# A three-stage transformer block in split fp32: the projections' first place from x without its tokens' scales, both norms' scales applied where it is emptied

## The reference

```python
    return rmsnorm(x, final_g)            # the end of first_block
...
def rms_norm(x, g):
    y = xf * lax.rsqrt(jnp.mean(xf * xf, axis=-1, keepdims=True) + NORM_EPS) * g.astype(jnp.float32)
...
        h = rms_norm(x, norm_mix_pre[l])
        proj = h @ w_in[l]
        q, k, v, p = jnp.split(proj, (D_ATTN, D_ATTN + D_KV, D_ATTN + 2 * D_KV), axis=-1)
...
        p_prev = jnp.concatenate([jnp.zeros_like(p[:, :1]), p[:, :-1]], axis=1)
        p = p + (p_prev - p) * rwkv_shift_mix[l]
```

## Time and profile before

| what | us |
|---|---|
| median of 3 runs | 2027.43 (2027.31 to 2029.51) |
| the profiled execution | 2027.34 |
| its span | 2026.0 |
| TensorE busy | 1829.3 (90% of the span) |
| VectorE busy | 1046.8 (52%) |
| ScalarE busy | 639.8 (32%) |
| GpSimd busy | 88.4 (4%) |
| granted TensorE clock, mean | 0.936 of full |

### The profile page before, as it was taken

One profiled execution on the slowest core, in us unless ns is written; L12 is line 12 of the kernel. 1 busy time (PEld: TensorE's weight loads), 2 busy tenths in 40 slices (PEclk: granted clock), 3 DMA queues, 4 the chain that ended last, 5 costly groups with the idle time before them and its releaser, 6 DMA issues.

```text
span 2026.0 us, 21412 instructions
## 1 busy us (share of the span) xinstructions
PE 1829.3 (90%) x8828; PEld 1473.9 (73%) x8828; DVE 1046.8 (52%) x1316; ACT 639.8 (32%) x786; POOL 88.4 (4%) x87
## 2 busy tenths in 40 slices
PE   5659999999997899999969979985599999999997
PEld 3238888887776688888857768874478888888885
DVE  4874674477426543244344574435566552466533
ACT  2124312421321342133224423432344431244422
POOL 2400010010000000000000120100000000000000
PEclk8769999999997899999988989997799999999997
DMA  9713464365321132232312240002122332332321
GB/s 357 266 63 112 155 225 153 103 209 197 94 83 42 62 105 91 96 104 84 104 62 73 63 115 8 4 1 62 42 83 87 101 104 84 103 104 84 104 83 42
DMA packets 123920, 208.55 MB, mean 103 GB/s; under 512 B 13885, under 2 KB 48341, under 8 KB 123824
## 3 DMA queue, kind: packets, MB, share of 16 engines
q1 hardware_dynamic: 115360, 174.94, 26.4%
q0 software_dynamic: 7792, 29.43, 4.4%
q10 hardware_dynamic: 672, 2.82, 0.4%
HBM read 204.01 MB, written 4.73 MB: 103 GB/s over the span
## 4 chain that ended last, share of the span: by engine, by line
PE 85%; DVE 10%; ACT 2%; issue 1%; DMA 1%; SPq 1%; DVEq 0%; ACTq 0%
PE bank L514 73%; DVE ada_acc L1569 2%; DMA ada_ring<-in_ada_w 1%; PE bank L843 1%; PE bank L530 1%; PE bank L826 1%; PE bank L806 1%; PE bank L525 1%; DVE gT L1852 1%; SPq L461 1%; DVE outer L1850 1%; PE bank L888 0%; PE bank L655 0%; DVE tmp L1531 0%; PE bank L867 0%
## 5 line engine op out<-in xcount | busy, mean ns | idle before, releaser
L1494 DVE TENSOR_TENSOR w_lo<-raw,w_hi 128x2048 fp32r<-128x2048 f32 x138 | 319.9, 2319 | 541.6 <-ACT w_hi L1103 541.6
L1103 ACT ACTIVATE w_hi<-raw 128x2048 fp32r<-128x2048 f32 x138 | 263.9, 1913 | 634.7 <-PE bank L514 611.2
L514 PE MATMUL bank<-h_hi,w_hi 128*128 128x512 f32 x736 | 292.5, 397 | 11.1 <-DVE h_lo L1541 7.7
L514 PE MATMUL bank<-u_hi,w_hi 128*128 128x512 f32 x768 | 300.5, 391 | 0.8 <-DVE conv L2047 0.8
L514 PE MATMUL bank<-u_hi,w_lo 128*128 128x512 f32 x768 | 299.0, 389 | 0.0
L514 PE MATMUL bank<-u_lo,w_hi 128*128 128x512 f32 x768 | 298.8, 389 | 0.0
L514 PE MATMUL bank<-h_lo,w_hi 128*128 128x512 f32 x736 | 290.2, 394 | 0.0
L514 PE MATMUL bank<-h_hi,w_lo 128*128 128x512 f32 x736 | 289.8, 394 | 0.0
L514 PE MATMUL bank<-f_hi,w_hi 128*128 128x512 f32 x512 | 200.3, 391 | 2.7 <-DVE f_lo L1544 2.4
L514 PE MATMUL bank<-f_lo,w_hi 128*128 128x512 f32 x512 | 199.7, 390 | 0.0
L514 PE MATMUL bank<-f_hi,w_lo 128*128 128x512 f32 x512 | 199.7, 390 | 0.0
(11 more groups left out here) (328 smaller groups left out, 2029.2 us busy)
## 6 DMA issues: line engine op xcount, KB each, us to landing
raw<-in_mlp_w SPq DMA_DIRECT2D x128, 512.0 KB, 4.6
raw<-in_w_ffn_up SPq DMA_DIRECT2D x64, 512.0 KB, 4.7
ada_ring<-in_ada_w POOLq DMA_DIRECT2D x24, 1024.0 KB, 5.8
ada_ring<-in_ada_w SPq DMA_DIRECT2D x9, 2048.0 KB, 13.9
raw<-in_w_ffn_down SPq DMA_DIRECT2D x32, 512.0 KB, 4.4
raw<-in_w_in SPq DMA_DIRECT2D x20, 512.0 KB, 4.4
raw<-in_sgu_w_in SPq DMA_DIRECT2D x16, 512.0 KB, 4.8
x_rows<-in_ada_w SPq DMA_DIRECT2D x3, 2048.0 KB, 12.9
```

Source lines behind the costliest of these rows:

```text
L514: mm = te.matmul(bank[:, n], a, b, start=first and k == 0 and j == 0, stop=last and k == 3 and j == 2)
L1103: se.activation(m.ring(s)[0], m.raw[:, slot], ACT.Copy).then_inc(sem("hi_made"), 1)
L1494: ve.tensor_tensor(lo, m.raw[:, slot], hi.bitcast(F32), ALU.subtract).then_inc(sem("lo_made"), 1)
```

## The change

Place 0 reads x * g1 * g2, split into h_hi and h_lo (`gained_hi`, `gained_lo`) as the MLP's last tiles are finished, and so needs neither scale. Squares of x and of x * g1 are summed side by side in that time (`second_square`, `add_second_square`, into the space of rstd_diag). Both means come after three quarters of slab 76 (`two_means`), the product of both scales is worked out in rows of four and spread inside slab 77 (`scale_spread`), and VectorE empties place 0 with it into bT (`scaled_out`), from which ScalarE and VectorE do the shift. For places 1 to 4, h is rebuilt over h_hi and h_lo from x, the gains and the product of scales; place 1 is now the one with k outermost. The first scale alone is spread in slab 78 and kept, and the rewriting of xT by NORM_FINAL (x_final) is done in the mixer's eight units.

The lora matrices get a place of their own and are loaded at the end of the MLP. `blocks(1)` comes in the middle of slab 82. The blocks are stored in two halves and loaded in two times four transfers, on SP's queue ahead of slab 86. The inverses are cut into six pieces between the shifts of places 3 and 4, and the product of r and the decays goes from GpSimd to VectorE (`r_decayed`).

```diff
--- before.py
+++ after.py
...
-    sy.wait_ge(sem("blocks_out"), 16)
...
-    for q in range(4):
-        sy.dma_start(m.ub[32 * q:32 * q + 32], t["blocks"][q].rearrange("s g t -> g s t")).then_inc(sem("blocks_in"), 16)
-    sy.wait_ge(sem("decayed"), 3)
+    for part in range(2):
+        sy.wait_ge(sem(f"blocks_out{part}"), 16)
+        for q in range(4):
+            a = 16 * part
+            sy.dma_start(m.ub[32 * q + a:32 * q + a + 16],
+                         t["blocks"][q, :, a:a + 16].rearrange("s g t -> g s t")).then_inc(sem("blocks_in"), 16)
...
+        if s == SLABS["w_out"]:
+            blocks_in(sy, t, m, sem)
...
-    mlp(1, NORM_MLP1, NORM_FINAL, m.u2_hi, m.u2_lo, m.sq_d)
-    norm_spread(NORM_FINAL)
-    norm_mean(NORM_PROJ, m.sq_d[:, 3])
-    norm_spread(NORM_PROJ)
...
+    mlp(1, NORM_MLP1, None, m.u2_hi, m.u2_lo, m.sq_d)
...
+    def two_means():
+        norm_mean(NORM_FINAL, m.sq_d[:, 3])
+        te.wait_ge(sem("second_added"), 7)
+        for j in range(4):
+            mm = te.matmul(bank[:, 4, 4 + j:5 + j], m.first_rstd[:, P * j:P * j + P], m.mean_ones[:, 0:1], start=True, stop=True)
+        mm.then_inc(sem("second_meaned"), 1)
+    def scale_spread():
+        te.wait_ge(sem("scale_diag"), MILESTONE["scale_diag"])
+        te.matmul(m.rstd_bank, ones[:, :], m.first_rstd, start=True, stop=True).then_inc(sem("scale_spread"), 1)
+    def first_spread():
+        te.wait_ge(sem("scale_copied"), MILESTONE["scale_copied"])
+        norm_spread(NORM_FINAL)
...
         te.wait_ge(sem("z_squashed"), 2)
...
+        te.wait_ge(sem("first_copied"), MILESTONE["first_copied"])
         for i in range(4):
...
-    beside = {(1, 0, 3): decays, (1, 1, 3): rates, (2, 0, 1): key_norms, (2, 0, 3): key_norms_back,
-              (2, 1, 3): lambda: blocks(0), (3, 0, 3): lambda: blocks(1)}
+    beside = {(0, 0, 2): two_means, (0, 1, 0): scale_spread, (1, 0, 1): first_spread, (1, 0, 3): decays, (1, 1, 3): rates, (2, 0, 1): key_norms, (2, 0, 3): key_norms_back,
+              (2, 1, 3): lambda: blocks(0), (3, 0, 1): lambda: blocks(1)}
...
-                normed(NORM_PROJ, 4 * k + kk)
+                if place == 0:
+                    te.wait_ge(sem("gained_hi"), 4 * k + kk + 1)
+                    te.wait_ge(sem("gained_lo"), 4 * k + kk + 1)
+                else:
+                    normed(NORM_PROJ, 4 * k + kk)
...
+                 before_k if place < 2 else None, before_n, k_outer=place == 1 and k == 0, after_n=after_n)
...
         for o in range(4, 8):
             emptied(g0 + 11, o - 4)
+            if layer:
+                gained_hi(o)
+            if layer and o == 7:
+                second_square(6)
             square(next_norm, o, m.xT[:, o], sq)
+            if layer and o != 6:
+                second_square(o)
+    def gained_hi(o):
+        se.activation(m.h_hi[:, o], m.xT[:, o], ACT.Copy, scale=m.gain[:, 40 + o:41 + o]).then_inc(sem("gained_hi"), 1)
+    def second_square(o):
+        if o >= 3:
+            se.wait_ge(sem("second_added"), o - 2)
+        place = m.tmp[:, (o - 1) % 2] if o else m.first_rstd
+        se.activation(place, m.xT[:, o], ACT.Square, scale=m.col("final_g", o)).then_inc(sem("second_squared"), 1)
...
+    split_to(SLABS["proj"] + 1)
+    se.wait_ge(sem("second_meaned"), MILESTONE["second_meaned"])
     root(NORM_FINAL)
-    for k in range(DT):
-        se.wait_ge(sem("x_final"), k + 1)
-        square(NORM_PROJ, k, m.xT[:, k], m.sq_d)
-    root(NORM_PROJ)
-    normalise_hi(NORM_PROJ, m.h_hi)
+    se.wait_ge(sem("second_mean_scaled"), MILESTONE["second_mean_scaled"])
+    se.activation(m.scale_rows[:, 1], m.scale_rows[:, 1], ACT.Sqrt, bias=m.eps[:, 0:1]).then_inc(sem("second_rooted"), 1)
+    split_to(SLABS["proj"] + 2)
+    se.wait_ge(sem("scale_spread"), MILESTONE["scale_spread"])
+    se.activation(m.scale[:, :], m.rstd_bank, ACT.Copy).then_inc(sem("scale_copied"), 1)
...
+            if place == 0:
+                emptied(GROUPS["proj"], n)
+                se.activation(dest[o], m.bT[:, n], ACT.Copy, scale=m.one_less[:, o - 6:o - 5]).then_inc(sem("shift_started"), 1)
...
-    split_to(first + 2)
-    empty(0, range(4))
-    emptied(GROUPS["proj"], 1)
+    for n in range(4):
+        normed_hi((n,))
+        empty(0, (n,))
+    se.wait_ge(sem("first_shifted"), 2)
     se.activation(m.zT[0:64, 0], m.zT[0:64, 0], ACT.Tanh).then_inc(sem("z_squashed"), 1)
     se.activation(m.zT[:, 1], m.zT[:, 1], ACT.Sigmoid).then_inc(sem("z_squashed"), 1)
+    normed_hi(range(4, 8))
     split_to(first + 3)
+    se.wait_ge(sem("spread"), NORM_FINAL + 1)
+    se.activation(m.first_rstd, m.rstd_bank, ACT.Copy).then_inc(sem("first_copied"), 1)
     decays()
...
+    def gained_lo(o):
+        ve.wait_ge(sem("gained_hi"), o + 1)
+        ve.scalar_tensor_tensor(out=m.h_lo[:, o], in0=m.xT[:, o], scalar=m.gain[:, 40 + o:41 + o], in1=m.h_hi[:, o].bitcast(F32),
+                                op0=ALU.mult, op1=ALU.subtract).then_inc(sem("gained_lo"), 1)
+    def add_second_square(o):
+        ve.wait_ge(sem("second_squared"), o + 1)
+        if o > 1:
+            ve.wait_ge(sem("second_added"), o - 1)
+        ve.tensor_tensor(m.first_rstd, m.first_rstd, m.tmp[:, (o - 1) % 2], ALU.add).then_inc(sem("second_added"), 1)
...
+    split_to(SLABS["proj"] + 1)
...
+    ve.wait_ge(sem("second_meaned"), MILESTONE["second_meaned"])
+    ve.tensor_tensor(rows, rows, bank[:, 4, 4:8], ALU.mult).then_inc(sem("second_mean_scaled"), 1)
+    ve.wait_ge(sem("second_rooted"), MILESTONE["second_rooted"])
...
+    def diagonal(a):
+        return ve.tensor_tensor(m.rstd_diag[:, :, :], ident.unsqueeze(1).broadcast_to([P, 4, P]),
+                                a.unsqueeze(2).broadcast_to([P, 4, P]), ALU.mult)
+    diagonal(rows).then_inc(sem("scale_diag"), 1)
...
+    def r_decayed():
+        for i in range(4):
+            ve.wait_ge(sem("dve_emptied"), EMPTIED[GROUPS["proj"] + 3][i][1])
+            ins = ve.tensor_tensor(m.rT[:, i], m.rT[:, i], m.cum[:, i], ALU.mult)
+        ins.then_inc(sem("r_decayed"), 1)
...
+    def inverses(high, low):
+        if high == 31:
+            ve.wait_ge(sem("blocks_in"), 128)
+            ve.wait_ge(sem("y_cleared"), 1)
+        for r in range(high, low - 1, -1):
...
+            if r < 31:
+                ve.wait_ge(own.sem, solved["n"])
...
+                solved["n"] = own.on(ins)
...
+    def scaled_out(n):
...
+        full(first + 1, GROUPS["proj"], n)
+        ve.tensor_tensor(m.bT[:, n], bank[:, n], m.scale[:, :], ALU.mult).then_inc(sem("dve_emptied"), 1)
...
+    def first_shift(n):
...
+        ve.wait_ge(sem("shift_started"), n + 1)
+        shifted["n"] += 1
+        ve.scalar_tensor_tensor(out=dest[o][:, 1:], in0=m.bT[:, n, 0:T - 1], scalar=m.col("rwkv_shift_mix_2", o - 6),
+                                in1=dest[o][:, 1:], op0=ALU.mult, op1=ALU.add).then_inc(sem("first_shifted"), 1)
...
+    def normed_scaled(k):
...
+        ve.scalar_tensor_tensor(out=m.tmp[:, k % 2], in0=m.xT[:, k], scalar=m.gain[:, 40 + k:41 + k], in1=m.scale[:, :],
+                                op0=ALU.mult, op1=ALU.mult).then_inc(sem("scaled"), 1)
...
+    def normed_lo(k):
...
+        ve.tensor_tensor(m.h_lo[:, k], m.tmp[:, k % 2], m.h_hi[:, k].bitcast(F32), ALU.subtract).then_inc(sem("normed_lo"), 1)
...
     first = SLABS["proj"]
     split_to(first + 2)
-    shift(0)
+    ve.wait_ge(sem("scale_copied"), MILESTONE["scale_copied"])
+    diagonal(first_rows).then_inc(sem("diag_made"), 1)
+    normed_scaled(0)
+    scaled_out(0)
+    scaled_out(1)
+    normed_scaled(1)
+    normed_lo(0)
+    scaled_out(2)
+    scaled_out(3)
+    normed_scaled(2)
+    normed_lo(1)
+    normed_scaled(3)
+    normed_lo(2)
+    first_shift(0)
+    first_shift(1)
+    normed_lo(3)
+    normed_scaled(4)
+    for k in range(4, DT):
+        if k + 1 < DT:
+            normed_scaled(k + 1)
+        normed_lo(k)
     split_to(first + 3)
+    first_shift(2)
+    first_shift(3)
     decays()
     split_to(first + 4)
...
-    shift(3)
+    shift(3, (0, 1))
+    inverses(31, 26)
+    shift(3, (2, 3))
     split_to(first + 9)
-    inverses()
-    shift(4)
+    r_decayed()
+    inverses(25, 15)
+    shift(4, (0,))
+    inverses(14, 12)
+    shift(4, (1,))
+    inverses(11, 9)
+    shift(4, (2,))
+    inverses(8, 6)
+    shift(4, (3,))
+    inverses(5, 1)
...
         take(u)
+        ve.scalar_tensor_tensor(out=m.xT[:, u], in0=m.xT[:, u], scalar=m.col("final_g", u), in1=m.first_rstd,
+                                op0=ALU.mult, op1=ALU.mult).then_inc(sem("x_final"), 1)
...
+    ge.wait_ge(sem("slab_used"), SLABS["proj"])
+    ge.dma_start(m.lora[0:64, :], t["w_decay_up_2"]).then_inc(sem("lora_in"), 16)
+    ge.dma_start(m.lora[64:128, :], t["w_iclr_up_2"]).then_inc(sem("lora_in"), 16)
...
-    ge.wait_ge(sem("blocks_copied"), 8)
-    ge.dma_start(t["blocks"].rearrange("q s g t -> (q s) g t"), m.lu).then_inc(sem("blocks_out"), 16)
...
```

(8 more changed lines are left out.)

127 lines of the change are left out of this document (80 added, 47 removed).

## The result

The changed kernel takes 2001.53 us (median of 4 runs, 1998.87 to 2002.7) beside 2027.37 us for the kernel before on the same chip: a ratio of 0.9869 with a 95% interval of 0.9855 to 0.9883. Its profiled execution took 2002.35 us with a span of 2000.9 us; the mean granted clock rose from 0.936 to 0.941. The forecast was 2000.7 us.

A forecast was written before the change was run, and what follows sets the result against it. TensorE was judged fed except in two holes: serial norms after the MLP, and the vvT wait behind VectorE's inverses. 2027.34 - 21.2 - 7.2 + 1.6 + 0.2 = 2000.7 us, range 1997 to 2003.

The forecast's parts named there:

- The hole between the MLP and the projections: From the MLP's end to slab 79: place 0's work fills TensorE's wait for two serial norms, gain 21.2 us.
- The stall before the decays: After slab 78: TensorE waits for ScalarE's copy of the first scale, 3.8 us of new stall.
- The decays at 3.70 us: Decay matmuls between slabs 78 and 79: they take 3.70 us, as before the change.
- The clock falls behind the stall too: Rival, at the decays: idleness lowers TensorE's clock there, up to 3.7 us more, 2004.4 us; chance 0.17.
- 1.6 us of low clock behind the means: Slab 76, after the one-column means: eight matmuls run at 0.43 and not 0.23, 1.6 us lost.
- The second stage, 7.2 us: From slab 82 to the vvT wait: earlier blocks and inverses, cheaper w_lo; TensorE starts at 1206.5 instead of 1213.7.
- I take no delay: Block loads before the inverses: eight half-size loads issued in 5.04 us, VectorE with 1.5 us of slack, no delay.
- the two larger terms: VectorE around slab 85: six inverse steps (3.6 us) run earlier; w_lo takes 2.3, not 5.88, with r's product 2.5.
- x_final hidden, xt in time, no wait of inverse_u for xt: Mixer: eight x_final pieces hide in VectorE's 4.80 us idle; inverses return about one microsecond before their first reader.
- The serialised loads: Rival, SP's queue: each of eight block loads drains before the next (6.0 us), giving 2038.7 us; chance 0.03.
- The table loads: Rival, ScalarE's tanh and sigmoid before the stall: each load holds twice its length, 2.6 us more, 2003.3; chance 0.03.
- The 0.2 us for the product of gains: Near the kernel's start: the extra product of gains costs 0.2 us, like any tiny VectorE piece.

The follow-up runs named there:

- means_first: Changed kernel with the two means and the spread of the scale ahead of place 0 instead of inside it: 2014.85 us, ratio to before 0.9935.
- warm_stall: Changed kernel with twelve unused matmuls filling TensorE's stall before the decays: 1998.19 us, ratio to before 0.9852.
- all_mended: Changed kernel with early first-scale copy, four full-size block loads, two r products before the inverses, five unused matmuls in the vvT wait: 1993.79 us.
- inverses_late: Changed kernel with VectorE's inverses in one piece behind the r products, and the last place's four shifts behind them: 2007.64 us, ratio to before 0.9895.
- r_on_pool: Changed kernel with r's product back on GpSimd, in one piece behind the last shift of place 3: 2004.06 us, ratio to before 0.9877.
- x_final_thrice: Changed kernel with each of the mixer's eight x_final products done three times on VectorE: 2000.45 us, ratio to before 0.9857.
- warm_values: Changed kernel with six unused matmuls in TensorE's wait for vvT: 2000.89 us, ratio to before 0.9868.

## Why the prediction was right, and where its steps failed

The total was off by 0.8 us, less than what runs of one kernel differ. The mechanisms of both stages were right. Two terms of the sum for the clock were wrong, in opposite directions, and so nearly cancelled. The steps, one by one:

- **The hole between the MLP and the projections.** Right in mechanism and in size: 21.2 us forecast less the 1.6 that the sum books apart for the clock at the means, so 19.6; measured 19.5 and 19.2 in the two pairs. The size hides the errors of the next points. TensorE went through slabs 76 to 78 without a wait; the end of slab 78 came 36.3 us behind the last xT, forecast 36.9. means_first shows the mechanism itself.
- **The stall before the decays.** Right: forecast 3.8 us, released by ScalarE's copy; measured 2.95, released by it.
- **The decays at 3.70 us.** This step failed. "The clock falls behind the stall too" stood among the rivals with a chance of 0.17 and up to 3.7 us; it happened: 7.04 and 7.16 us, so 3.4 more, and 1.4 to 1.6 us more in the first matmuls of slab 79. The argument against it, that the means "still ran at 1.24" behind the first wait of the old hole, misread that row. The same eight took 0.94 us at the full clock (changed kernel) and 1.86 at the half rate (means_first), so 1.24 is a row in which the clock fell: the granted clock is 0.78 from 1046.10 to 1047.50 and 0.50 from there to 1050.80. The next row of the same trace, which the prediction does not show, is at the half rate; two such matmuls take 1.02 at the full one:

```profile
1048.70 2.07 PE L530 MATMUL bank<-rstd_diag,ones 128*128 128x512 f32 x2 [1.29 <-DVE rstd_diag L1511]
```

  So the old trace already had a wait of 3.83 us with the half rate behind it, and spoke for the rival.
- **1.6 us of low clock behind the means.** This failed too, to the other side: 0.94 and 1.03 us for eight matmuls each, 1.7 us from the first to the next full matmul where the sum had 2.5, and 0.39 to 0.49 for each matmul behind them. Nearest rows were not near: there 32 narrow matmuls stood in a row, here twice eight among full ones.
- **These two offset each other**, together with a shorter stall and one more item that was not in the sum. The old key norms were followed by eight matmuls of 0.6 us, 1.5 us lost in all. The prediction read that dip, used it as the price of the means and let it stand at the key norms. Nothing of the kind is there in the changed kernel, on the same 3.63 us of narrow matmuls:

```profile
1112.64 3.63 PE L772 MATMUL bank<-const,bonus 128*128 128x2 f32 x32
1116.13 0.48 PE L531 MATMUL bank<-h_hi,w_hi 128*128 128x512 f32 x1
```

  The dip is in both profiles of before and in neither of the changed kernel. It comes back in warm_stall and all_mended, so it was not a certain gain; whether chance or what went before decides it is open. The real balance against the sum is +3.4 and about +1.5 for the clock at the decays, and -0.8 in the means, -1.6 behind them, -1.5 at the key norms and -0.9 at the stall: some 4.9 us of errors one way and 4.8 the other. That the forecast came so close is luck.
- **The second stage, 7.2 us.** Right: the wait for vvT fell by 6.8 and 7.5 us. w_lo of slab 85 took 2.28 (forecast 2.3), the r products 2.49 (2.5). "I take no delay" for the loads of the blocks failed by a microsecond: the eight were issued in 9.04 us and not in 5.04, the last came 2.85 us after VectorE asked, some 1.5 were slack as forecast, and w_lo started 73.7 us behind slab 79's first matmul and not 72.6 as before. inverses_late and r_on_pool bear out the two larger terms, each above its forecast: +5.4 to +6.2 and, without the longer wait for the blocks, +1.9 (forecast +4.6 and +1.1).
- **x_final hidden, xt in time, no wait of inverse_u for xt.** Right; x_final_thrice shows the first, and for the others TensorE waits for no transfer from value_rows to 1260 us.
- **The rivals.** The serialised loads did not come near: eight in 9.04 us with 2.8 of waiting in it, against the 4.6 per load from which they would have decided. The table loads cost 1.28 each. The 0.2 us for the product of gains was not tried alone; it is below what these runs tell apart.

## What to carry to other kernels

When a hole on the bounding engine is closed, look at what the helpers have queued by then: here one 0.58 us copy behind a 1.9 us split cost 5.3 us up to the next slab, 1.8 of it waiting and the rest in clock, and putting it two pieces earlier was worth nearly a quarter of the whole change by the medians. Before a row is used against a loss of clock, hold its duration against the same instructions at both rates: 1.24 us looked like the usual cost of the means, and was a clock that was just falling. A stall on TensorE has two prices, its length and the half rate behind it, and the second can be the larger; put both in the sum. Splitting a transfer to start it earlier only pays where the first part can go and the queue is not held by the pieces; time the whole set, not the start.

## What the runs showed of the hardware that was not expected

- **The clock after short idleness.** 2.95 us without work, and the eight decay matmuls took 7.04 to 7.16 us in eight profiles; with filler or without the wait 3.67 to 3.70 in four. Yet waits of 5.6 to 13.8 us for vvT were followed by one spell or by two, in no order of their length, and the same narrow matmuls of the key norms (3.63 to 3.75 us) were followed by the lower clock in four profiles of fourteen. One wait's aftermath does not foretell another's.
- **Filler moves a spell as well as prevents it.** It won 3.4 us before dense work (warm_stall) and nothing before thin work (warm_values).
- **GpSimd beside VectorE.** The same 128x2048 product took 4.62 us on GpSimd in the kernel before and 6.50 in r_on_pool, and VectorE's neighbour grew by 3.6 us (2.29 to 5.88) and by 4.4 us (0.33 to 4.76). The length of the neighbour did not matter, but the order of the starts did: the later one waited out the earlier, GpSimd's too (a copy of 0.23 us took 2.29).
- **Loads of many small rows.** The four loads took 5.04 us to issue in the kernel before and 2.96 us here, with a median landing of 6.0 and 3.5 us. One of the four alone took 3.46 us to issue there, and no wait stands in the rows. The row of before was no price of the load alone; what else was in it stays open.
